# One query-tile loop of sparse attention: GpSimd takes weight scaling from ScalarE, short units share a PSUM bank, scores run on half rows

## The chip, the core and the metric

The kernel runs on one core of a Trainium2 chip. The metric is the device time of one execution in microseconds (us). Five engines work side by side and meet at semaphores: TensorE (PE in the profile, its weight loads as PEld), VectorE (DVE), ScalarE (ACT), GpSimd (POOL) and SyncE (SP), which issues most transfers.

## The reference

A two-layer decoder trunk over 256 tokens of width 1024. The first layer is a gated linear recurrence with a dense SwiGLU; the second is sparse attention with three branches (compressed, selected, window) and a top-2-of-8 expert SwiGLU. Here only the attention of the second layer matters:

```python
lc = einsum('bghqd,bgnd->bghqn', qi, k_cmp) + bias      # compressed keys, 15 of them
o_cmp = masked_softmax(lc, ...) @ v_cmp
ls = einsum(qi, ks) + bias                               # selected blocks: with 256 tokens all of them
o_slc = masked_softmax(ls, dist >= 0) @ vs
lw = einsum(qi, kw) + bias_w                             # window of 512: all earlier tokens
o_win = masked_softmax(lw, ...) @ vw
return gq[..., 0:1] * o_cmp + gq[..., 1:2] * o_slc + gq[..., 2:3] * o_win
```

There are 16 heads of 64 channels in 4 groups; the 4 heads of a group share keys and values. The gates `gq` are sigmoids of a projection of the normed input. The result goes through an output projection (called `mixB` in the kernel), is added to the residual, and the expert layer follows.

## The kernel before, in words

Everything but the expert stage is straight code; each engine has its own instruction list, in an order written by hand, and `then_inc`/`wait_ge` on semaphores are the only ties. PSUM has 8 banks; `job_table` gives each product its bank and its turn in it. `free_bank` waits until the previous job of the bank has been emptied, `filled` waits for a job's product, `evacuated` waits until a job's bank was emptied.

The attention is cut into 32 units `units[u] = (tt, h)`, a head h of one tile of 128 queries. `ORDER` takes the second tile first, so units 0 to 15 are long (256 keys) and units 16 to 31 short (128 keys). For each unit both the selected and the window branch are computed. The steps:

- `scores(u)` on TensorE: one product of 128 rows, `QT[:, h//2]` against `KTZ[h % 2]`. A column block of QT holds two heads, 64 rows each; KTZ[0] has the keys in rows 0 to 63 and zeros below, KTZ[1] (in the tile silu_g) the other way round. The product has 512 columns in a long unit and 256 in a short one. The banks of L rotate over three.
- `biased(s)` on VectorE: the add of the bias out of PSUM into `LB` (line 1486), the row maximum (1489), its sign (1490).
- ScalarE: two exponentials with their sums (1144), one for each branch.
- VectorE: the reciprocal times the gate gives `RW` (1557, 1558, `weight_ready`).
- The scaling of the exponentials by RW: branch 0 on ScalarE (1153), branch 1 on GpSimd (809).
- `turned(u)` on TensorE: 4 transposes of 128 columns in a long unit, 2 in a short one (1913), into job ("PT", u), in banks 2 and 3 by turns.
- ScalarE copies that bank to `PTB` (1160).
- `values(u)` on TensorE for two units at once: the compressed part (`VCZ` against `PCT`), then 16 instructions on 64 columns each in a long pair, 8 in a short one, into the bank of OT. The two heads of a pair go to the two halves of the output rows.

TensorE's list takes units in pairs. In the step for an even s: `scores(s)`, `scores(s+1)`; the compressed scores of a tile if its turn has come (`CMP_AT` is 2 for the long tile and 10 for the short one, here at `CMP_AT - 2`); `turned(s-4)`, `turned(s-3)`; `values(s-6)`. ScalarE's list in step s: both exponentials of unit s, the scaling of unit s-1, the copy of unit s-4. VectorE's: `biased(s)`, compressed work where it is due, the weight of unit s-1.

Ahead of the loop TensorE projects keys, values and queries, sums the query squares (`qsum`), makes the hidden layers of the two compressions (`hid` 0 and 1, of 7.2 us each), the scores of units 0 and 1, the gates' projection (32 products into the bank "gate"), and then small products for the compressed keys (`kc`, `kcsum`) and values (`vc`). VectorE turns the gates into sigmoids (1497, 1498), spreads vc into `VCZ` (1502) and kc into `KCZ` (1511). The compressed scores wait for KCZ (`norm_b`, 5).

After the loop ScalarE moves the last bank of OT (`heads_out`, 912), then, when all four are empty, makes `x_hi` in four pieces (956); VectorE makes `x_lo`; TensorE starts `mixB`, whose first sweep waits for x_hi piece by piece.

Of the kernel before, what the change touches and what calls it, by code (L numbers as in the profile page):

```python
# [29 lines left out]
ALU = mybir.AluOpType  # L30
# [116 lines left out]

def job_table():
# [48 lines left out]
    for br in (1, 2):  # L197
        job(("k", br))
        job(("v", br))
        job(("ksum", br))  # L200
    for b in range(4):
        job(("qB", b))
    for b in range(4):
        job(("qsum", b))
    for s in range(2):
        job(("hid", s))
    job(("gate",))
    job(("kc",))
    job(("vc",))
    job(("kcsum",))  # L210
# [3 lines left out]
    for u in range(TT * HB):  # L214
        job(("L", u), (0, 1, 4)[u % 3])
        job(("PT", u), 2 + u % 2)
# [54 lines left out]
def trunk(nc, ins, out):  # L271
# [5 lines left out]
    with ctx:  # L277
# [89 lines left out]
        VCZ = between[0:ROWS_C, 0, 0:HB // 2 * P].rearrange("p (j n) -> p j n", j=HB // 2)  # L367
        gates = area(15244, TT, 3 * HB)
        qsq = silu_g
        KTZ = [KT, silu_g[:, :, :].rearrange("p (b g) t -> p b g t", b=2)]  # L370
# [355 lines left out]
        def _(pool):  # L726
# [70 lines left out]
            pool.wait_ge(norm_b, 4)  # L797
            for br in range(2):
                pool.dma_start(by_parity(KTZ[1], high, br, 0), by_parity(KT, low, br, 0)).then_inc(keys_copied, 16)
                pool.dma_start(by_parity(KTZ[1], high, br, 1), by_parity(KT, high, br, 1)).then_inc(keys_copied, 16)  # L800
            pool.wait_ge(keys_zero, 1)
            pool.memset(KTZ[1][low], 0.0).then_inc(keys_zero, 1)
            pool.wait_ge(keys_copied, 16 * 6)
            pool.memset(KTZ[0][high], 0.0).then_inc(keys_zero, 1)
# [111 lines left out]
        def _(act):  # L916
# [161 lines left out]
            for br in (1, 2):  # L1078
# [16 lines left out]
                act.activation(ksq[br - 1], ksq[br - 1], ACT.Exp, scale=-0.5).then_inc(rs_b, 1)  # L1095
            for b in range(4):
# [10 lines left out]
            for b in range(4):  # L1107
                evacuated(act, ("qsum", b))
                v = qsq[:, 2 * b:2 * b + 2, :]
                act.activation(v, v, ACT.Exp, scale=-0.5).then_inc(rs_b, 1)  # L1110
            act.preload_act_table_set("gelu_apprx_tanh_and_others")
            for s in range(2):
# [9 lines left out]
                if s == 0:  # L1122
                    for b in (1, 2, 3):
                        refill(make_hi, act, ("qB", b))
            act.preload_act_table_set("natural_log_exp_and_others")
            k = filled(act, ("gate",))
            for tt in range(TT):
                last = act.activation(gates[:, tt, :], ps[:, k, 3 * HB * tt:3 * HB * tt + 3 * HB], ACT.Exp, scale=tok_minus[:, tt:tt + 1])
            last.then_inc(bank_free[k], 1)
# [3 lines left out]
            k = filled(act, ("kcsum",))  # L1133
            act.activation(kcsq, ps[:, k, 0:G * NCMP], ACT.Ln, bias=eps[:, :], scale=1.0 / DH).then_inc(bank_free[k], 1)
            evacuated(act, ("kcsum",))
            act.activation(kcsq, kcsq, ACT.Exp, scale=-0.5).then_inc(rs_b, 1)

            for s in range(len(units) + LAG):
                if s < len(units):
                    w = P * (units[s][0] + 1)  # L1140
                    act.wait_ge(row_max, s + 1)
                    for br in range(2):
                        v = LB[:, s % KEPT, br, 0:w]
                        act.activation(v, v, ACT.Exp, bias=RM[:, s, br:br + 1], accum_out=RS[:, s, br:br + 1]).then_inc(exp_done, 1)  # L1144
                if s in CMP_AT:
# [3 lines left out]
                if 1 <= s <= len(units):  # L1149
# [4 lines left out]
                if s >= LAG:  # L1154
                    u = s - LAG
                    n = 2 * (units[u][0] + 1) * P
                    k = filled(act, ("PT", u))
                    if u >= 4:
                        pv_release(act, u - 4)
                    act.activation(PTB[:, u % 4, 0:n], ps[:, k, 0:n], ACT.Copy).then_inc(bank_free[k], 1)  # L1160
                    if u % 8 == 7 and u > 8:
                        heads_out(act, u // 8 - 1)
            heads_out(act, 3)
            for b in range(4):
                for n in range(4):
# [990 lines left out]
```

## Time and profile before

| what | value |
|---|---|
| median of 3 runs | 1557.31 us (1555.98 to 1561.93) |
| the profiled execution's own time | 1557.5 us |
| its span in the trace | 1555.7 us |
| TensorE / VectorE / ScalarE / GpSimd busy | 96% / 77% / 65% / 9% |
| attention loop, first compressed score to last value product | about 475 to 545.5 us of the span |
| expert stage | from about 590 us to the end |

Times in the rows are microseconds from the start of the span. A busy TensorE is not TensorE at its peak, and the ends of matmuls are modelled; the starts of weight loads tell its pace better. In the chain of work, each row is a piece of the path that ended last, and "x20" is how many instructions were merged.

### The profile page before, as it was taken

The numbers are of one execution on the slowest core, as the hardware profiler recorded it, in microseconds if no ns is written. First come the engines' busy times: TensorE is split into PE (matmuls) and PEld (weight loads), VectorE is DVE, ScalarE is ACT, GpSimd is POOL, SyncE is SP. The second block draws the span as 40 slices with busy tenths as digits, with TensorE's granted clock in tenths as the row PEclk, the third lists the DMA queues.
The fourth block names the chain that finished last, engine by engine and source line by source line (L and its number), as shares of the span: only waits on it lengthen the run. The fifth ranks groups of instructions, "written<-read, shape, count | busy, mean of one in ns | idle before, by whom it ended". The sixth has DMA issues, their size and how long they took to land.

```text
span 1555.7 us, 22749 instructions
## 1 busy us (share of the span) xinstructions
PE 1497.7 (96%) x8592; PEld 1302.9 (84%) x8592; DVE 1199.5 (77%) x1039; ACT 1018.5 (65%) x1005; POOL 141.4 (9%) x145
## 2 busy tenths in 40 slices
PE   8998999999998889999999999999999999999995
PEld 7998899998996687888888888888888888888884
DVE  6854455556457747888888888898898988888887
ACT  5743443435545936778777777777777777777775
POOL 0600100000212309100000000000000000001000
PEclk9999999999998989999999999999999999999998
DMA  9760345556986018999999999999999999999993
GB/s 301 230 204 1 111 163 181 193 177 173 199 245 261 1 55 298 414 399 387 389 375 391 381 373 387 380 375 382 383 381 379 385 372 383 388 373 379 410 376 113
DMA packets 176873, 456.92 MB, mean 294 GB/s; under 512 B 11220, under 2 KB 72877, under 8 KB 176819
## 3 DMA queue, kind: packets, MB, share of 16 engines
q1 hardware_dynamic: 171234, 436.29, 75.9%
q0 software_dynamic: 5408, 19.73, 4.9%
q8 instruction: 38, 0.62, 0.2%
q10 hardware_dynamic: 176, 0.14, 0.0%
q14 instruction: 17, 0.13, 0.0%
HBM read 437.52 MB, written 16.78 MB: 292 GB/s over the span
## 4 chain that ended last, share of the span: by engine, by line
PE 91%; ACT 3%; DVE 2%; DMA 2%; issue 1%; POOL 0%; ACTq 0%; POOLq 0%; DVEq 0%
PE ps L1668 88%; PE ps L2064 2%; DMA ring<-in_moe_w_gu 1%; ACT arena L1144 1%; ACT x_hi L937 0%; PE ps L2130 0%; DVE w_lo L558 0%; DVE arena L1489 0%; DVE arena L1486 0%; DMA arena<-item_rows,arena 0%; ACT between L1160 0%; PE ps L1913 0%; DMA arena<-in_norm_mix_g 0%; ACT arena L1153 0%; ACT w_hi L554 0%
## 5 line engine op out<-in xcount | busy, mean ns | idle before, releaser
L558 DVE TENSOR_TENSOR w_lo<-ring,w_hi 128x2048 fp32r<-128x2048 f32 x339 | 774.0, 2291 | 108.2 <-ACT w_hi L554 107.1
L554 ACT ACTIVATE w_hi<-ring 128x2048 fp32r<-128x2048 f32 x339 | 651.0, 1920 | 237.7 <-PE ps L1668 231.1
L1668 PE MATMUL ps<-w_hi,x_hi 128*128 128x512 f32 (+1 forms) x1056 | 336.9, 383 | 2.7 <-DVE x_lo L1567 2.7
L1668 PE MATMUL ps<-w_hi,x_lo 128*128 128x512 f32 (+1 forms) x1056 | 333.6, 380 | 0.0
L1668 PE MATMUL ps<-w_lo,x_hi 128*128 128x512 f32 (+1 forms) x1056 | 284.0, 380 | 0.0
L1668 PEld LDWEIGHTS ps<-w_hi,x_lo 128*128 128x128 f32 x1056 | 198.7, 188 | 37.6
L1668 PEld LDWEIGHTS ps<-w_lo,x_hi 128*128 128x128 f32 x1056 | 198.6, 188 | 37.6
L1668 PEld LDWEIGHTS ps<-w_hi,x_hi 128*128 128x128 f32 x1056 | 196.3, 188 | 39.5 <-issue 4.4
L507 DVE TENSOR_TENSOR w_lo<-ring,w_hi 128x2048 fp32r<-128x2048 f32 x67 | 153.2, 2291 | 82.4 <-ACT w_hi L501 82.3
L501 ACT ACTIVATE w_hi<-ring 128x2048 fp32r<-128x2048 f32 x67 | 127.5, 1910 | 101.0 <-PE ps L1668 97.7
L1668 PE MATMUL ps<-w_hi,hid 128*128 128x512 f32 x768 | 191.6, 391 | 0.4 <-DVE hid L1625 0.4
L1668 PEld LDWEIGHTS ps<-w_hi,hid 128*128 128x128 f32 x768 | 142.9, 188 | 29.8 <-DVE hid L1625 0.8
L1668 PE MATMUL ps<-x_hi,w_hi 128*128 128x256 f32 x800 | 115.0, 296 | 12.2 <-ACT x_hi L937 6.1
L1668 PEld LDWEIGHTS ps<-x_hi,w_hi 128*128 128x128 f32 x800 | 105.4, 200 | 19.4 <-issue 13.5
L1668 PE MATMUL ps<-x_lo,w_hi 128*128 128x256 f32 x800 | 105.7, 286 | 0.0
L1668 PE MATMUL ps<-x_hi,w_lo 128*128 128x256 f32 x800 | 104.2, 283 | 0.0
L1668 PE MATMUL ps<-w_lo,hid 128*128 128x512 f32 x384 | 102.8, 389 | 0.0
L1668 PEld LDWEIGHTS ps<-x_lo,w_hi 128*128 128x128 f32 x800 | 101.5, 195 | 0.0
L1668 PEld LDWEIGHTS ps<-x_hi,w_lo 128*128 128x128 f32 x800 | 99.6, 192 | 0.1
L1668 PEld LDWEIGHTS ps<-w_lo,hid 128*128 128x128 f32 x384 | 72.1, 188 | 15.0
L889 POOL DMA_DIRECT2D item_rows<-arena x8 | 4.4, 550 | 848.7 <-ACT arena L1225 848.7
L1668 PE MATMUL ps<-hid,w_hi 128*128 128x256 f32 x352 | 63.8, 283 | 0.0
(266 smaller groups left out, 1209.2 us busy)
## 6 DMA issues: line engine op xcount, KB each, us to landing
ring<-in_moe_w_gu SPq DMA_DIRECT2D x224, 1024.0 KB, 6.6
ring<-in_moe_w_down SPq DMA_DIRECT2D x112, 1024.0 KB, 6.6
ring<-in_ffn_w_gu SPq DMA_DIRECT2D x22, 1024.0 KB, 5.1
ring<-in_a_w_in SPq DMA_DIRECT2D x16, 1024.0 KB, 11.3
ring<-in_ffn_w_down SPq DMA_DIRECT2D x11, 1024.0 KB, 5.0
ring<-in_w_kv SPq DMA_DIRECT2D x6, 1024.0 KB, 5.3
item_rows<-hT SPq DMA_DIRECT2D x12, 512.0 KB, 11.7
ring<-in_a_w_out SPq DMA_DIRECT2D x4, 1024.0 KB, 5.4
```

The lines of the kernel that those rows point to most:

```text
L501: eng.activation(w_hi[:, m, :], src, ACT.Copy).then_inc(hi_ready[m], 1)
L507: eng.tensor_tensor(w_lo[:, m, :], ring[:, RAW[name][0], :], w_hi[:, m, :].bitcast(F32), ALU.subtract).then_inc(lo_ready[m], 1)
L554: eng.activation(w_hi[:, m % PAIRS, :], ring[:, m % RING, :], ACT.Copy).then_inc(hi_ready[m % PAIRS], 1)
L558: eng.tensor_tensor(w_lo[:, m % PAIRS, :], ring[:, m % RING, :], w_hi[:, m % PAIRS, :].bitcast(F32), ALU.subtract).then_inc(lo_ready[m % P ...
L889: pool.dma_start(item_rows.ap()[bass.ds(i, 1)].rearrange("o p d -> p (o d)"), yt).then_inc(rows_kept, 16)
L1144: act.activation(v, v, ACT.Exp, bias=RM[:, s, br:br + 1], accum_out=RS[:, s, br:br + 1]).then_inc(exp_done, 1)
L1668: return pe.matmul(o, w, x, start=start, stop=stop, **kw)
L2064: last = pe.transpose(ps[:, b, P * c:P * c + P], HM[:, at:at + P], ident)
```

## The change

1. **Scaling.** `both_on_pool(u)` is true for odd long units and for all short ones. There GpSimd scales both branches and ScalarE none. Even long units stay as they are.
2. **Turned weights.** Two short units share one PT bank (`turned_with`), half a bank each, and ScalarE empties it with one copy of 512 columns instead of two of 256. Banks 2 and 3 alternate between pairs.
3. **Scores.** No zero-padded keys any more. `scores(u)` issues two products of 64 rows, one for each head of a pair, on rows 0 to 63 and 64 to 127, after waiting for both L banks. GpSimd's four key copies are issued in `KT` itself right after the keys are scaled; two memsets of 64 x 2048 and the wait for `norm_b` go.
4. **Gates early.** The gate projection moves ahead of the query projection; its exponential and sigmoid follow there. ScalarE's three weight copies for mixB move ahead of the compression's activations.
5. **Order at the loop's start.** The scores of units 0 and 1 come between the two hidden layers. `biased(0..2)` are interleaved with `make_lo`. KCZ is made at VectorE's step 1, VCZ at step 4. ScalarE's part for kcsum comes after the exponentials of unit 0. Compressed scores are issued at `CMP_AT` instead of `CMP_AT - 2`.
6. **End.** x_hi pieces 0 and 1 are made before the last `heads_out`; TensorE no longer waits for all OT banks.

```diff
+def turned_with(u):
+    return u - u % 2 if ORDER[u // HB] == 0 else u
+def both_on_pool(u):
+    return ORDER[u // HB] == 0 or u % 2 == 1
...
-        job(("PT", u), 2 + u % 2)
+        if turned_with(u) == u:
+            job(("PT", u), 2 + (u // 2 if ORDER[u // HB] == 0 else u) % 2)
...
+                pool.dma_start(by_parity(KT, high, br, 0), by_parity(KT, low, br, 0)).then_inc(keys_copied, 16)
             for u, (tt, h) in enumerate(units):
                 pool.wait_ge(weight_ready, u + 1)
-                v = LB[:, u % KEPT, 1, 0:P * (tt + 1)]
-                pool.tensor_scalar(v, v, RW[:, u, 1:2], None, ALU.mult).then_inc(p2_ready, 1)
+                for br in (0, 1) if both_on_pool(u) else (1,):
+                    v = LB[:, u % KEPT, br, 0:P * (tt + 1)]
+                    pool.tensor_scalar(v, v, RW[:, u, br:br + 1], None, ALU.mult).then_inc(p2_ready, 1)
...
-                if 1 <= s <= len(units):
+                if 1 <= s <= len(units) and not both_on_pool(s - 1):
...
+                    elif u % 2 == 1:
+                        k = filled(act, ("PT", u - 1))
                         pv_release(act, u - 4)
+                        act.activation(PTB[:, u % 4 - 1:u % 4 + 1, 0:T], ps[:, k, :].rearrange("p (u n) -> p u n", u=2), ACT.Copy).then_inc(bank_free[k], 1)
...
+            def scores(u):
+                tt, h = units[u]
+                w = P * (tt + 1)
+                pe.wait_ge(norm_b, h // 4 + 1)
+                for n in range(2):
+                    free_bank(pe, ("L", u + n))
+                for n in range(2):
+                    half, b = slice(DH * n, DH * n + DH), J[("L", u + n)][0]
+                    mm(ps[:, b, 0:2 * w].rearrange("p (b t) -> p b t", b=2), QT[half, h // 2, P * tt:P * tt + P],
+                       KT[half, 0:2, h // HP, 0:w], True, True).then_inc(bank_full[b], 1)
...
+                if s == 0:
+                    pe.wait_ge(keys_copied, 16 * 4)
+                    scores(0)
...
-                    if s == CMP_AT[tt] - 2:
+                    if s == CMP_AT[tt]:
```

## Rows read from the trace of the kernel before

**Rows 1.** The page: the chain that ended last, shares of the span by engine.
```profile
PE 91%; ACT 3%; DVE 2%; DMA 2%; issue 1%; POOL 0%; ACTq 0%; POOLq 0%; DVEq 0%
```

**Rows 2.** Busy time by stretch: PE, PEld, DVE, ACT, POOL, then granted clock, DMA, GB/s.
```profile
475.00:483.00 8.00, 7.93 (x23) 5.03 (x24) 4.59 (x14) 2.74 (x10) 0.94 (x1) 0.57 1.03 419
...
488.00:519.00 31.00, 27.54 (x203) 19.03 (x202) 24.17 (x75) 26.01 (x84) 12.63 (x14) 0.98 0.11 45
519.00:546.00 27.00, 22.18 (x183) 16.65 (x181) 17.34 (x72) 23.75 (x95) 9.07 (x15) 1.00 0.00 1
```

**Rows 3.** The chain of work around the loop's start: start, length, what.
```profile
425.89 45.58 PE ps L1668 x358
...
475.07 4.76 PE ps L1668 x18
```

**Rows 4.** Timeline at the head: start, length, engine, line.
```profile
466.17 0.64 ACT L1119 ACTIVATE arena<-ps 128x240 f32<-128x240 f32 x2 [1.48 <-PE ps L1668]
466.82 1.28 ACT L1125 ACT_TABLE_LOAD   x1
467.79 3.54 PEld L1668 LDWEIGHTS ps<-w_gate,hT 128*128 128x128 f32 x31 [0.24 <-issue]
473.05 1.29 DVE L1502 TENSOR_TENSOR between<-ps,const 120x512 f32<-120x512 f32 x2
474.25 0.56 DVE L1511 SCALAR_TENSOR_TENSOR arena<-arena,cols 64x60 f32<-64x60 f32 x2
```

**Rows 5.** The chain of work among the long units.
```profile
488.30 0.61 DVE arena L1486
...
489.86 1.10 ACT arena L1144 x4
490.96 0.40 ACT arena L1153
491.36 0.49 ACT between L1160
...
491.98 0.63 PE ps L1913 x4
492.61 4.86 PE ps L1668 x38
```

**Rows 6.** Timeline of the same stretch.
```profile
490.00 0.69 DVE L1486 TENSOR_TENSOR arena<-ps,arena 128x512 f32<-128x512 f32 x1
492.76 0.85 PEld L1668 LDWEIGHTS ps<-between,arena 128*64 128x64 f32 x16
494.95 0.69 DVE L1486 TENSOR_TENSOR arena<-ps,arena 128x512 f32<-128x512 f32 x1 [1.27 <-PE ps L1668]
```

**Rows 7.** The chain of work among the short units.
```profile
529.28 0.29 ACT arena L1153
529.57 0.28 ACT between L1160
...
529.98 0.41 PE ps L1913 x2
530.39 1.46 PE ps L1668 x12
531.87 0.44 DVE arena L1486
```

**Rows 8.** Timeline, VectorE, the add of unit 23.
```profile
527.22 0.42 DVE L1486 TENSOR_TENSOR arena<-ps,arena 128x256 f32<-128x256 f32 x1
```

**Rows 9.** Groups by line and form, 488 to 545 us: busy, mean ns, idle before.
```profile
L809 POOL TENSOR_SCALAR arena<-arena 128x256 f32<-128x256 f32 x13 | 12.0, 925 | 18.4 <-DVE arena L1558 18.4
L809 POOL TENSOR_SCALAR arena<-arena 128x128 f32<-128x128 f32 x16 | 9.7, 605 | 14.9 <-DVE arena L1558 14.9
```

**Rows 10.** Timeline behind the last value product.
```profile
545.51 0.60 ACT L912 ACTIVATE xn<-ps 128x512 f32<-128x512 f32 x1 [0.92 <-PE ps L1668]
...
547.43 3.25 PEld L1668 LDWEIGHTS ps<-x_hi,w_hi 128*128 128x128 f32 x14 [0.16 <-ACT x_hi L956]
```

More of the change, by code:

```diff
@@ L200, in job_table @@
         job(("ksum", br))
+    job(("gate",), 5)
     for b in range(4):
@@ L1095, in _ @@
                 act.activation(ksq[br - 1], ksq[br - 1], ACT.Exp, scale=-0.5).then_inc(rs_b, 1)
+            k = filled(act, ("gate",))
+            for tt in range(TT):
+                last = act.activation(gates[:, tt, :], ps[:, k, 3 * HB * tt:3 * HB * tt + 3 * HB], ACT.Exp, scale=tok_minus[:, tt:tt + 1])
+            last.then_inc(bank_free[k], 1)
             for b in range(4):
@@ L1546, in _ @@
                     dve.tensor_copy(PCT[:, tt, :, :], ps[0:ROWS_C, k, 0:T].rearrange("p (a t) -> p a t", a=2)).then_inc(bank_free[k], 1)
-                if 0 < s < len(units):
+                if s == 1:
+                    dve.wait_ge(rs_b, 7)
+                    evacuated(dve, ("kc",))
+                    dve.wait_ge(keys_zero, 1)
+                    for par in range(2):
+                        half = slice(DH * par, DH * par + DH)
+                        last = dve.scalar_tensor_tensor(KCZ[half, :, par, :], KCT[half].rearrange("p (g n) -> p g n", g=G), cols[half, ROW_K:ROW_K + 1],
+                                                        kcsq[half].rearrange("p (g n) -> p g n", g=G), ALU.mult, ALU.mult)
+                    last.then_inc(norm_b, 1)
+                if s == 4:
+                    k = filled(dve, ("vc",))
+                    wide = [ROWS_C, HB // 2, DH]
+                    for a in range(2):
+                        last = dve.tensor_tensor(VCZ[:, 4 * a:4 * a + 4, :].rearrange("p j (r d) -> p (j r) d", r=2),
+                                                 ps[0:ROWS_C, k, DH * a:DH * a + DH].unsqueeze(1).to_broadcast(wide),
+                                                 K("own")[0:ROWS_C].unsqueeze(2).to_broadcast(wide), ALU.mult)
+                    last.then_inc(bank_free[k], 1)
+                if 2 < s < len(units):
                     biased(s)
@@ L1558, in _ @@
                     dve.tensor_tensor(RW[:, u, :], RW[:, u, :], gates[:, tt, 3 * h + 1:3 * h + 3], ALU.mult).then_inc(weight_ready, 1)
-            for n in range(4):
-                evacuated(dve, ("OT", n))
+            pv_release(dve, len(units) - 3)
             input_lo(OT)
@@ L1864, in _ @@
                 mm(ps[:, b, :], halves, ksq[br - 1], True, True).then_inc(bank_full[b], 1)
+            pe.wait_ge(gate_folded, 1)
+            b = free_bank(pe, ("gate",))
+            for tt in range(TT):
+                for k in range(KC):
+                    last = mm(ps[:, b, 48 * tt:48 * tt + 48], hT[:, k, P * tt:P * tt + P], w_gate[:, k, :], k == 0, k == KC - 1)
+            last.then_inc(bank_full[b], 1)
             dense("qB")
@@ L1980, in _ @@
                     values(s - LAG - 2)
-            for n in range(4):
-                evacuated(pe, ("OT", n))
             def logits(ks):
```

142 lines of the change are left out of this document (52 added, 90 removed).

## The prediction

> **What bounds the kernel now.** I read the page first, for the chain that ended last. It is TensorE for nine tenths of the span [rows 1]. So only what lengthens or shortens TensorE's chain counts, and the expert stage, from 590 us on, is untouched: whatever the attention gains arrives at the end one for one, because the expert weights' stream is released by the same chain. Then the chain of work in order of time, which says where TensorE is not alone. Up to the loop's start it is one piece of TensorE work, 45.58 us long [rows 3]. At the start and inside the loop it goes through all four engines. Third, the busy time by stretch: between 488 and 546 us no engine is full. TensorE is busy 27.5 of 31 us and 22.2 of 27, VectorE 24.2 and 17.3, and the granted clock is 0.98 and 1.00 [rows 2]. A loop in which nobody is full is bound by a ring of waits, so I looked for the ring.
>
> **The ring of the long units.** It reads off the chain and the timeline. The add of unit 5 starts at 488.3; its exponentials take 489.86 to 490.96, then ScalarE's queue gives the scaling of unit 4 (0.40) and the copy of unit 1 (0.49) [rows 5]. That copy frees the PT bank for `turned(3)`, at 491.98 (0.63), which is followed in TensorE's list by `values(0)` and `scores(8)`, and the add of unit 8 starts at 494.95 [rows 5, 6]. So three units cost 6.7 us; one more unit of VectorE's own pace is 1.7 us (488.3 to 490.0) [rows 5, 6], and the ring returns to the same parity after 8.4 us for four units, 2.1 us each.
>
> **The ring of the short units** is the same. The add of unit 23 is at 527.22 [rows 8]; the scaling (0.29) and copy (0.28) end at 529.85, `turned` is at 529.98 (0.41), values and scores take 1.46, and the add of unit 26 starts at 531.87 [rows 7]: 4.65 us for three units. VectorE's pace for a short unit I estimate, from the add's 0.44 against 0.69 and the long 1.7 [rows 6, 7], as 1.3.
>
> **The change, part by part.**
>
> *Scaling moved to GpSimd.* ScalarE loses 8 scalings of 0.40 and 16 of 0.29 [rows 5, 7], 7.8 us of work. In a long ring the scaling on the path is that of an even unit (unit 4 above, and it repeats with step 2), and even units keep it on ScalarE. So of the long 3.2 us nothing comes off the path; they were cover only. In the short ring the 0.29 does come off. What is late next is GpSimd: an odd long unit takes 2 x 0.93 = 1.85 us, a short one 2 x 0.605 = 1.21 [rows 9]. The long unit's `turned` then waits for: add of unit 2 places on, + 1.8 for its pace and the weight, + 1.85 + 0.1. Followed by turned, values and scores (3.0, from 491.98 to 494.95 [rows 5, 6]) that is 6.75 us for four units against the ring's 8.4: hidden. In the short ring: 1.3 + 1.21 + 0.1 + 1.9 (529.98 to 531.87 [rows 7]) = 4.5 against about 5.5: hidden too. GpSimd would set the pace only if a scaling took over (8.4 - 6.75)/2 = 0.8 us more than now. Two scalings in a row have no row; I take twice one, with bounds of the same and 1.5 times.
>
> *Shared PT bank.* In short units `turned` of a pair no longer waits for the copy three steps ahead, but `values`, behind it in the same list, still does. So the wait moves over one step: `turned` (0.41) leaves the path, and a copy of 512 columns (0.49 against 0.28 [rows 5, 7]) enters it. With the scaling: 0.29 + 0.41 - 0.2 = 0.5 us for each turn of four units. Sixteen short units are four turns: -2.0 us if all of it counts, 0 if VectorE or GpSimd takes over at once. VectorE is close behind, so I take -1.6.
>
> *Split scores.* Two products of 64 rows replace two of 128. There is no such product in the trace. The nearest row is `values`, where 16 loads on alternating column halves start in 0.85 us, 0.053 each [rows 6], while the four full transposes of a unit take 0.63 [rows 5]. Bounds for a long pair: full overlap saves half of it, none saves nothing; I take overlap of neighbours, a quarter, 0.4 us. The ring waits only for the first product of the pair, and that is not shortened at all. The saving lies in TensorE's slack: worth 0 in the rings, some tenths where TensorE alone is the path.
> The Trainium skill, TensorEngine Tiling (Array Packing), Key Properties, says that tiles work independently, and that changing the tiling mode drains the array. By its first half a long pair would save a half, by the second each pair pays one drain more; on the ring both change the sum by less than 0.5 us, and no row here shows a drain of this kind by itself.
>
> *Compressed scores two units later.* Those of the short tile now stand on the path: the 4.86 us piece with 38 instructions is values(0), two score products and 16 compressed ones [rows 5], of which the 16 are some 1.8. Issued at unit 10 instead of 8, they lie beside VectorE's unit 10 (1.7) and stick out by perhaps 0.5 beyond the two scores ahead of them. -1.3 us, bounds 0 and -1.8.
>
> *Loop start.* The gates' 3.5 us of loads [rows 4] move ahead of the queries: TensorE was the path there and is again, so 0. kc would start at 471.3 as before. But hidden layer 1 now ends last, directly before it: its activation (0.64) and a table load (1.28 [rows 4]), which lay under the gates' products, come onto the path of kcsum. Then ScalarE does unit 0's exponentials (1.1 [rows 5]) before kcsum's two operations, and VectorE adds unit 2 (1.7) before KCZ (0.56 [rows 4]). From 471.3: 0.7 + 1.3 + 0.2 for the square, 0.5 for the kcsum product, 1.1 for scores of unit 2, 1.7, 0.6 gives the compressed scores at 477.4, against 475.07 [rows 3]. There they ran at a granted clock of 0.57 [rows 2] and with two score products took 4.76 [rows 3], after some 2 us of waiting; the new order waits as long, so I take the low clock again: 3.4 for 16, end at 480.9, against 479.8. After that VectorE has unit 2 behind it (-1.6), but VCZ (1.29 [rows 4]) before unit 4. Net 1.1 - 1.6 + 1.3 = +0.8. Bounds: -0.7 if the clock stays up there (16 products at full clock save 1.5), +3 if the third weight copy of mixB, now ahead of the activation in ScalarE's list, waits for its transfer. Half of GpSimd's copies and both memsets go; nothing on the path waited for them.
>
> *End.* Behind the last value product come heads_out at 545.51, x_hi and the first sweep's loads until 550.7, 0.23 each [rows 10]. Four of these 16 products and two x_hi pieces no longer follow heads_out: -1.0, bounds 0 and -2.
>
> **The sum.** +0.8 - 1.3 - 1.6 - 1.0 = -3.1 us. Against the profiled execution's own 1557.5 (span 1555.7 and 1.8 around it), which is 0.2 above the median of the runs, that is 1554.4.
>
> **Rivals.**
> *VectorE's floor.* If relief of ScalarE and TensorE dissolves both rings, VectorE runs without gaps. It idles 6.8 + 9.7 us in the two stretches [rows 2], some 5 of it behind its last unit; 11 less, with +0.8 and -1.0 outside, is -11: 1546.3. For it: the wait between engines is a few tenths in each ring. Against it: the long ring keeps all its links. 0.10.
> *The change does nothing measurable in sum*: the start costs more (up to +3) or GpSimd's pairs and the extra drain eat the short ring's 0.5, -1 to +3 us: 1556.5 to 1560.5. For it: nearly every step leaves a new wait behind the old. 0.23.
> *The clock falls inside the loop* (the other side). TensorE does less in the same time, with more gaps. At 475 to 483 us the clock was 0.57 after such a gap [rows 2]. TensorE's part of each turn of four units is 3.0 us long and 1.9 short [rows 5 to 7]; at half clock it doubles: 11 long units and 16 short ones cost 8.2 + 7.6 = 15.8 more, less the 3.1: up to 1570. It decides when a fifth of the loop (3.1/15.8) runs at 1.2 GHz, and is over 0.5% slower from 0.7 of it on. Against it: now the clock holds at 0.98 to 1.00 with visible gaps. 0.07.
> The Trainium skill, TensorE: Matmul & The Clock Gate, HAM oscillation, has the same mechanism, bursts with waits between them that fall back to the low clock each time; the trace agrees for the loop's start only.
>
> **How the numbers follow.** My forecast, -1 to -7.8 us, has 0.60. The measurement tells 0.5%, 7.8 us, from no change. Faster by more: the floor rival and the forecast's edge, 0.12. Slower by more: the clock rival's worst part, 0.04. Within: 0.84. The range takes the forecast, most of the nothing case and the near end of the floor rival: 1548.5 to 1560.
>
> **What would show it.** In the changed profile: the long ring still 2.1 us a unit with ScalarE idle before the exponentials; short adds about 1.4 us apart; the loop's first four units no earlier than before; unit 10 not delayed by compressed scores; the first mixB product starting before x_hi is whole. Score loads of a pair starting a quarter sooner, not half. GpSimd busy 8 x 0.93 + 16 x 0.605 = 17 us more, never what `turned` waits for. I am wrong if `turned` waits for GpSimd, if VectorE shows no gaps, or if the clock reads below 0.9 between 488 and 540.

## The result: 10 us faster, 7.2 us more than forecast

The changed kernel takes 1547.0 us (median of 11 runs, 1546.4 to 1552.3) against 1557.3 (11 runs, 1554.1 to 1561.9). The ratio is 0.9935, 95% interval 0.9926 to 0.9944: faster by 0.65%. The forecast was 1554.4, its range 1548.5 to 1560.0, with 0.12 for faster by over 0.5%. The time lies outside the range. Eight of the eleven runs lie between 1546.4 and 1547.8, the other three 2 to 5 us above.

The profiled execution's span is 1545.4 us, 10.3 less than before. The table follows the same event through both traces. A step's share is the difference between its own lead and the lead of the row above.

| event (start) | before | after | lead | forecast for the step | measured |
|---|---|---|---|---|---|
| add of unit 5 (loop's start is behind) | 488.2 | 484.7 | 3.5 | +0.8 | -3.5 |
| add of unit 12 (compressed scores behind) | 506.8 | 501.5 | 5.3 | -1.3 | -1.8 |
| add of unit 31 (short ring behind) | 539.1 | 531.5 | 7.5 | -1.6 | -2.2 |
| first of the 64 products behind mixB (the end is behind) | 569.0 | 559.5 | 9.5 | -1.0 | -2.0 |
| end of the span | 1555.7 | 1545.4 | 10.3 | 0 | -0.8 |

Counted from the first piece of x_hi for the queries instead of the span's start, unit 5 came 4.1 us nearer (65.7 us before, 61.6 after): this trace of the changed kernel reached that piece 0.6 us later than the one before.

So three fifths of the error, 4.3 of 7.2 us, were made before unit 5. Read the chain of work there first (start, length, what was on the path):

```profile
414.93 53.78 PE ps L1677 x428
...
468.74 0.63 ACT arena L1128 x2
...
469.39 1.28 ACT L1131
...
470.95 1.50 PE ps L1677 x5
...
472.48 0.70 DVE arena L1497
...
474.66 1.98 PE ps L1677 x16
...
476.67 0.56 DVE arena L1516
```

TensorE now runs in one piece from before 414.93 to 468.71. Before, the piece that I had read as the whole head began at 425.89 [rows 3]. This is the chain of the kernel before just ahead of that row:

```profile
422.19 0.47 ACT arena L1086
422.65 3.19 ACT x_hi L937 x8
```

For 4 us the path went through ScalarE, which made x_hi for the query projection. The busy times of 422 to 426 us say what TensorE did meanwhile (PE, PEld, DVE, ACT, POOL, then clock, DMA share, GB/s), first before, then after:

```profile
422.00:426.00 4.00, 2.23 (x9) 1.01 (x8) 2.45 (x7) 4.00 (x11) 0.00 (x0) 1.00 1.04 348
```

```profile
422.00:426.00 4.00, 4.00 (x33) 3.52 (x32) 2.07 (x6) 3.59 (x10) 0.55 (x1) 1.00 1.04 347
```

One quarter of the loads' time was used, and now nearly all of it: the 32 gate products fall exactly into this hole. From the first x_hi piece to the first query sum it was 25.6 us (422.55 to 448.18) and is 26.4 (423.14 to 449.55). The gates cost 0.8 us in their new place; in the old one they took 3.9 (467.36 to 471.25, the next product).

VectorE at the loop's start (timeline: start, length, idle time in brackets):

```profile
461.45 0.69 DVE L1497 TENSOR_TENSOR arena<-ps,arena 128x512 f32<-128x512 f32 x1 [1.18 <-PE ps L1677]
465.17 0.68 DVE L1497 TENSOR_TENSOR arena<-ps,arena 128x512 f32<-128x512 f32 x1
472.48 0.69 DVE L1497 TENSOR_TENSOR arena<-ps,arena 128x512 f32<-128x512 f32 x1 [3.50 <-PE ps L1677]
```

Units 0 and 1 are done under the second hidden layer, and unit 2 before the compressed scores; the add of unit 3 follows at 478.3 (483.0 before). The adds of units 0 to 2 used to start at 467.7, 474.8 and 479.9.

The granted clock around the compressed scores (474.66 to 476.64 in the changed kernel), first in the changed kernel, then in two of the experiments below, act_scales and copy_first, which have the same order up to there:

```profile
474.00:476.00 2.00, 1.34 (x12) 1.34 (x13) 0.91 (x5) 0.97 (x4) 0.90 (x1) 1.00 1.03 420
```

```profile
474.00:476.00 2.00, 0.12 (x1) 0.12 (x1) 1.89 (x6) 0.68 (x4) 0.00 (x0) 0.63 1.04 424
```

```profile
474.00:476.00 2.00, 0.05 (x1) 0.05 (x1) 1.89 (x6) 0.76 (x4) 0.00 (x0) 0.65 1.03 420
```

In the changed kernel the clock fell as well, but behind the 16 products: it is 0.54 from 476 to 482 us. In the other two it had fallen before them, and they took 3.6 us instead of 2.0.

The stretches of [rows 2] after the change:

```profile
475.00:483.00 8.00, 5.38 (x27) 3.76 (x27) 6.02 (x17) 3.49 (x11) 3.69 (x4) 0.59 1.03 421
488.00:519.00 31.00, 26.51 (x248) 19.23 (x250) 25.80 (x85) 25.00 (x82) 19.83 (x25) 1.00 0.11 42
519.00:546.00 27.00, 22.21 (x183) 16.68 (x182) 16.14 (x60) 17.74 (x60) 14.50 (x25) 1.00 0.00 1
```

Still no engine is full between 488 and 519 us. The long ring has the same links as [rows 5], and its units are no nearer (unit 5 to unit 8: 6.7 us before, 6.8 after):

```profile
486.43 1.09 ACT arena L1141 x4
487.52 0.40 ACT arena L1155
487.92 0.49 ACT between L1162
...
488.54 0.63 PE ps L1925 x4
489.17 2.31 PE ps L1677 x22
```

In the short ring the scaling and `turned` of [rows 7] are gone, and the copy is the long one:

```profile
522.31 0.57 ACT arena L1141 x3
522.88 0.49 ACT between L1166
...
523.51 1.30 PE ps L1677 x11
...
524.83 0.43 DVE arena L1497
```

Behind the loop GpSimd has entered the chain, with the four scalings of the last pair:

```profile
533.02 2.35 POOL arena L812 x4
...
535.50 0.42 PE ps L1925 x2
```

mixB's first loads start before x_hi is whole; the timeline shows two of them, and then the run behind the third piece of x_hi, 10 loads of 0.13 us. Before they took 0.23 [rows 10], at a granted clock of 0.52 (547.43 to 550.68):

```profile
537.87 0.30 PEld L1677 LDWEIGHTS ps<-x_hi,w_hi 128*128 128x128 f32 x2 [0.38 <-issue]
...
540.05 1.26 PEld L1677 LDWEIGHTS ps<-x_hi,w_hi 128*128 128x128 f32 x10 [0.22 <-ACT x_hi L959]
```

From the add of the last unit to that run it is 8.5 us, as before (8.4). The end's 2.0 us come out of the run: four products fewer in it, 0.5, and the rest the clock, which is 1.00 here.

### The profile page after: what moved, and what is told of

Its sections match the earlier page's. It is cut to its first block, busy times and chain, and to the rows that moved or that the text cites. A ratio compares the mean times of both kernels' runs of the same rounds, so it can differ in the third digit from the quotient of the medians.

```text
span 1545.4 us, 22764 instructions
## 1 busy us (share of the span) xinstructions
PE 1486.9 (96%) x8592; PEld 1293.8 (84%) x8592; DVE 1200.6 (78%) x1039; ACT 1010.6 (65%) x973; POOL 152.7 (10%) x165
## 4 chain that ended last, share of the span: by engine, by line
PE 93%; DVE 2%; ACT 2%; issue 1%; DMA 1%; POOL 0%; ACTq 0%; POOLq 0%; DVEq 0%
PE ps L1677 91%; PE ps L2076 2%; DVE arena L1500 1%; DVE arena L1497 0%; PE ps L2142 0%; ACT arena L1141 0%; DMA arena<-item_rows,arena 0%; DMA arena<-in_norm_mix_g 0%; ACT x_hi L940 0%; PE ps L1688 0%; PE ps L1925 0%; ACT x_hi L970 0%; DVE arena L1501 0%; ACT between L1162 0%; POOL arena L812 0%
## 5 line engine op out<-in xcount | busy, mean ns | idle before, releaser
L1677 PEld LDWEIGHTS ps<-x_hi,w_hi 128*128 128x128 f32 x800 | 103.7, 197 | 15.7 <-issue 10.3
```

What stands on the lines that cost most here:

```text
L1677: return pe.matmul(o, w, x, start=start, stop=stop, **kw)
```

## The experiments

Two things make single spans poor witnesses here. The first piece of x_hi for the queries starts between 420.0 and 424.6 us from execution to execution, and what lies behind the stretch used here takes 985.0 to 988.9 us. So I compare the part between: from that x_hi piece to the first of the 64 products behind mixB ("the stretch"), 146.4 us before, 136.4 after. The ratios are to the kernel before, each with its 95% interval. The unit steps are starts of VectorE's adds.

| kernel | median (range, runs) | ratio | stretch, us |
|---|---|---|---|
| gates_late | 1549.2 (1547.4-1551.4, 4) | 0.9939 [0.9916, 0.9962] | 139.5 |
| before_gates_early | 1557.1 (1551.2-1559.5, 10) | 0.9990 [0.9975, 1.0005] | 146.6 |
| before_split | 1558.2 (1556.6-1560.4, 12) | 0.9995 [0.9986, 1.0005] | 148.4 |
| before_split_gates | 1556.1 (1550.8-1558.6, 12) | 0.9979 [0.9962, 0.9996] | 142.9 |
| scores_late | 1553.4 (1551.3-1555.8, 11) | 0.9967 [0.9951, 0.9982] | 142.9 |
| scores_full_late | 1555.0 (1550.9-1558.2, 12) | 0.9973 [0.9956, 0.9990] | 147.5 |
| scores_full | 1566.5 (1565.4-1568.2, 4) | 1.0049 [1.0032, 1.0066] | 157.3 |
| act_scales | 1549.6 (1547.4-1552.3, 4) | 0.9938 [0.9921, 0.9955] | 141.1 |
| pt_alone | 1547.9 (1546.9-1552.2, 4) | 0.9938 [0.9918, 0.9958] | 137.2 |
| cmp_early | 1554.8 (1548.4-1558.3, 10) | 0.9972 [0.9956, 0.9988] | 140.6 |
| tail_old | 1549.9 (1549.5-1551.9, 4) | 0.9949 [0.9932, 0.9965] | 139.4 |
| copy_first | 1548.0 (1541.2-1549.1, 4) | 0.9918 [0.9889, 0.9948] | 134.7 |
| best1 | 1544.3 (1540.6-1546.6, 6) | 0.9907 [0.9891, 0.9923] | 132.1 |
| best2 | 1543.0 (1542.1-1547.1, 6) | 0.9910 [0.9894, 0.9925] | 132.6 |

### The gates, taken out of the change and put alone into the kernel before

gates_late is the changed kernel with the gates' products, exponential and sigmoid behind the hidden layers; before_gates_early is the kernel before with them ahead of the queries (and with the banks that the changed kernel gives the small products around them). The diff shows TensorE's part of the first.

```diff
-            pe.wait_ge(gate_folded, 1)
-            b = free_bank(pe, ("gate",))
...
             dense("qB")
...
+            pe.wait_ge(gate_folded, 1)
+            b = free_bank(pe, ("gate",))
...
             evacuated(pe, ("hid", 0))
```

> The changed kernel with the gates' 32 products, their exponential and their sigmoid put back behind the hidden layers. Theory A (the gates' products fill the gap in which TensorE waits for ScalarE's x_hi pieces at 422 to 426 us, and that is where most of the gain at the loop's start is from): TensorE idles there again and the 3.5 us of loads stand behind the hidden layers again, so 3 to 5 us slower than the changed kernel, 1550 to 1552. Theory B (the gain at the loop's start is from the order of the small steps for the compressed keys, and from the unit sums already made): under 1 us slower, below 1548.

> The kernel before with nothing changed but the gates, whose products, exponential and sigmoid go ahead of the query projection. Theory A: 2.5 to 3.5 us faster than before, 1554 to 1555, with no gap in TensorE's work at 422 to 426 us. Theory B: within 1 us of before.

Taken out of the change, the gates cost 2.8 us up to the first small product behind the hidden layers (kc, 48.1 us behind x_hi instead of 45.3), and that is what the hole at x_hi is worth. The whole stretch is 3.2 us longer. The 0.4 between the two is a balance: the way from kc to the compressed scores is 1.1 us shorter (5.1 for 6.2), and these then took 3.5 us instead of 2.0. By the medians it is 2.2 us, less than the 3 to 5 expected, and the interval of the ratio is too wide to tell it from the changed kernel's 0.9935. Put alone into the kernel before, the gates give nothing (+0.2). The timeline of before_gates_early shows the second bound behind the first:

```profile
466.90 1.80 POOL L804 MEMSET arena<- 64x2048 f32 x1 [5.09 <-DMA silu_g<-arena]
...
468.93 0.30 PEld L1668 LDWEIGHTS ps<-arena 128*128 128x128 f32 x2 [1.56 <-issue]
468.96 1.13 PE L1668 MATMUL ps<-arena 128*128 128x512 f32 x2 [1.46 <-POOL arena L804]
```

TensorE is at `scores(0)` before the zero-padded keys are ready: they wait for a key copy, then a memset. In the kernel before the same memset ended at 465.74, 0.2 us ahead of the scores (465.96), and 0.2 us is also what lies between its end and them here (468.70 to 468.93), so there was nothing to spare. Behind this wait TensorE ran at 0.50 from 470 to 473 us, where the kernel before had 1.00, and the way from kc to the compressed scores took 5.1 us instead of 3.8: the 1.1 us left at kc went there. What follows: the gates' gain needs the new keys as well.

### The split scores, alone and with the gates

before_split is the kernel before with the split scores and their keys; before_split_gates has the early gates as well.

```diff
-        KTZ = [KT, silu_g[:, :, :].rearrange("p (b g) t -> p b g t", b=2)]
...
-            pool.wait_ge(norm_b, 4)
-            for br in range(2):
-                pool.dma_start(by_parity(KTZ[1], high, br, 0), by_parity(KT, low, br, 0)).then_inc(keys_copied, 16)
-                pool.dma_start(by_parity(KTZ[1], high, br, 1), by_parity(KT, high, br, 1)).then_inc(keys_copied, 16)
-            pool.wait_ge(keys_zero, 1)
-            pool.memset(KTZ[1][low], 0.0).then_inc(keys_zero, 1)
-            pool.wait_ge(keys_copied, 16 * 6)
-            pool.memset(KTZ[0][high], 0.0).then_inc(keys_zero, 1)
+                pool.dma_start(by_parity(KT, high, br, 0), by_parity(KT, low, br, 0)).then_inc(keys_copied, 16)
...
-                b = free_bank(pe, ("L", u))
-                mm(ps[:, b, 0:2 * w].rearrange("p (b t) -> p b t", b=2), QT[:, h // 2, P * tt:P * tt + P],
-                   KTZ[h % 2][:, 0:2, h // HP, 0:w], True, True).then_inc(bank_full[b], 1)
+                for n in range(2):
+                    free_bank(pe, ("L", u + n))
+                for n in range(2):
+                    half, b = slice(DH * n, DH * n + DH), J[("L", u + n)][0]
+                    mm(ps[:, b, 0:2 * w].rearrange("p (b t) -> p b t", b=2), QT[half, h // 2, P * tt:P * tt + P],
+                       KT[half, 0:2, h // HP, 0:w], True, True).then_inc(bank_full[b], 1)
```

> The kernel before with only the split scores: two products of 64 rows for each pair, four key copies, no padded keys and no memsets; gates and everything else as before. Theory (split scores and early gates pay only together): alone they save the half of a pair where TensorE is alone on the path, at the loop's start and ahead of the short tile's compressed scores, 0.8 us each, and nothing in the rings: 1555 to 1557 against 1557.3. First mixB load 1 to 2 us nearer to the start of x_hi than the 124.4 of before. Rival (each score product saves by itself in the rings too): 16 pairs at 0.8 and 0.1 us, 4 us or more, under 1553.5.

> The kernel before with the split scores and the early gates, nothing else. The gates alone gave 1557.1 (0.999). Theory (the padded keys were the second bound behind the gates): with both, TensorE neither stands at x_hi nor waits for the keys, so the 3.1 us of the gap at x_hi come on top of the split scores: 1552 to 1554, 3 us below the run with split scores alone, and the first mixB load 4 to 5 us nearer to x_hi's start than in the kernel before. Rival (parts are independent, gates are worth nothing at this place): the same time as with split scores alone.

The distance from x_hi to the first small product behind the hidden layers (kc) is the cleanest measure, because no ring lies in it, and low clock only in before_gates_early's last 0.8 us: 48.7 us before, 47.6 with the gates alone, 48.2 with the split alone, 45.3 with both, 45.3 in the changed kernel. Alone they save 1.1 and 0.5, together 3.4: the coupling is shown there. At mixB it is 5.5 us between the stretches of the split alone and of both, more than the 3 expected; the trace of the split alone has more time at the low clock behind unit 5 (below), and what each wait did to that was not separated. By the ratios the gates alone give 1.6 us, the split alone 0.8 and both 3.3. Only the last is clear of the kernel before, and none of it tells a coupling from a sum.

With the split alone the saving did not reach mixB, and the time did not change: the expected 1 to 2 us nearer fell, the rival's 4 us even more. The trace of before_split has a lower clock where the kernel before has 1.00, and the adds from unit 12 to unit 18 take 15.5 us instead of 12.4:

```profile
504.00:512.00 8.00, 7.38 (x56) 5.37 (x56) 5.85 (x19) 5.78 (x18) 2.77 (x3) 0.79 0.01 2
512.00:519.00 7.00, 5.49 (x38) 4.43 (x39) 3.40 (x13) 5.18 (x19) 2.45 (x3) 0.76 0.01 1
```

### The scores of units 0 and 1 between the hidden layers

scores_late is the changed kernel with the edit below in TensorE's list. scores_full has the padded keys and full products of the kernel before (the split of the last diff undone), with `scores(0)` left between the layers; scores_full_late has both edits.

```diff
-                if s == 0:
-                    pe.wait_ge(keys_copied, 16 * 4)
-                    scores(0)
+            pe.wait_ge(keys_copied, 16 * 4)
+            scores(0)
             evacuated(pe, ("hid", 0))
```

> The changed kernel with zero-padded keys and products of 128 rows again (with the copies and memsets that they need). Theory A (the pair's saving lies in TensorE's slack): 0 to 1 us slower, 1547 to 1548. Theory B (the saving of some 0.8 us for each long pair counts): 16 pairs, 4 to 8 us slower.

> The changed kernel with the scores of units 0 and 1 issued behind hidden layer 1 instead of between the two hidden layers; nothing else. Theory (TensorE is the path up to the small compressed products and the early scores only fill it in another order): the loop's start loses only what VectorE did under hidden layer 1, its add and maximum of units 0 and 1, about 3.5 us of work of which 1 to 2 us come on the path of unit 5: 1548 to 1549. Rival (the order at the start hides the low clock and VectorE's queue altogether): 3 us or more, 1550 and above. First small product (kc) 45.3 us behind x_hi's start as in the changed kernel by both.

> The previous kernel with full products of 128 rows against zero-padded keys (their four more copies and two memsets with them). Compared with the previous one it prices the split scores alone. Theory (half rows save a half of each pair, but in the rings only where TensorE is the path; the padded keys hold TensorE 1 to 2 us at the loop's start): 2 to 4 us above the previous kernel, 1550 to 1553. Rival (split scores are worth what the earlier test showed, 19 us, wherever scores(0) stands): 1562 or more.

scores_late costs 6.5 us of the stretch and 6.4 by the medians (5.0 by the ratios); 5.2 of the 6.5 lie before unit 5. My theory gave 1 to 2 and is wrong; its rival (3 and more) is right. VectorE's timeline says why: with the scores late, it does the adds of units 0 to 2 and two w_lo pieces in one row up to 479 us, and the compressed keys (L1546) stand behind them.

```profile
470.00 0.69 DVE L1497 TENSOR_TENSOR arena<-ps,arena 128x512 f32<-128x512 f32 x1 [8.33 <-PE ps L1677]
...
471.52 2.29 DVE L516 TENSOR_TENSOR w_lo<-ring,w_hi 128x2048 fp32r<-128x2048 f32 x1
...
475.24 2.28 DVE L516 TENSOR_TENSOR w_lo<-ring,w_hi 128x2048 fp32r<-128x2048 f32 x1
...
478.99 0.57 DVE L1546 SCALAR_TENSOR_TENSOR arena<-arena,cols 64x60 f32<-64x60 f32 x2
```

VectorE idled 8.33 us before the first of these rows. From kc to the compressed scores it is 9.7 us (469.89 to 479.61) instead of 6.2 (468.49 to 474.66), and then they run at the low clock, 0.50, after TensorE had waited 7 us.

scores_full_late against scores_late prices the half-row products together with their keys, everything else equal: 4.6 us of the stretch, 2.2 of it before unit 5 (all of it before unit 0: the hidden layers' end waits for the padded keys) and 1.7 between units 5 and 31; by the medians 1.6, by the ratios 0.9, with intervals that overlap. So 1 to 5 us, and that the two kernels differ is not shown by their times. Both expectations for scores_full, 0 to 1 and 4 to 8 us, missed by far: it is 19.5 us slower by the medians. But its 20.9 us of the stretch are no price of the products. In its trace TensorE stands 7.4 us between the hidden layers for the padded keys, and the second layer's 63 loads then take 13.6 us, half the pace, where it is 7.2 in the kernel before; the granted clock from 471.3 to 484.9 us is 0.50:

```profile
467.76 2.05 PE L1685 MATMUL ps<-arena 128*128 128x512 f32 x2 [7.43 <-issue]
...
471.31 13.56 PEld L1685 LDWEIGHTS ps<-arena,ring 128*128 128x128 f32 x63 [0.52 <-issue]
```

The early scores pay only because the unpadded keys are ready then: with padded keys the early ones are worse than the late ones (157.3 against 147.5).

### The short ring: scaling and shared bank

act_scales leaves all scaling of branch 0 with ScalarE (first function); pt_alone gives each short unit its own bank and copy again (second).

```diff
 def both_on_pool(u):
-    return ORDER[u // HB] == 0 or u % 2 == 1
+    return False
 def turned_with(u):
-    return u - u % 2 if ORDER[u // HB] == 0 else u
+    return u
```

> The changed kernel with all scalings of branch 0 back on ScalarE, as before the change; the shared bank, the split scores and the orders stay. Theory A (in short units ScalarE's scaling stands in the ring, in long ones it does not): adds of the short units 0.1 to 0.15 us further apart, 1 to 2 us slower in the loop, but the end behind the last unit shorter by about 1 us since GpSimd's four scalings of the last pair no longer stand on the path: 1547 to 1548. Theory B (ScalarE's relief is what brought both rings down): long units slower too, 1550 or more.

> The changed kernel with one PT bank and one copy for each short unit again. Theory A (the shared bank takes the transposes out of the ring): short adds 0.1 us or more further apart, 1.5 to 2.5 us slower, 1548.5 to 1549.5. Theory B (GpSimd's scaling did it, the bank does nothing): within 0.5 us of 1547.0.

Unit 15 to unit 31 takes 26.2 us before, 24.0 after, 24.9 in act_scales and 25.1 in pt_alone. The parts give 0.9 and 1.1 us, 2.0 of the 2.2 measured. The rest of act_scales' 4.8 us lies where its clock is lower: 1.6 before unit 5 (the 16 compressed scores, above), 1.3 between units 5 and 15 (0.79 between 490 and 498 us) and 0.9 behind unit 31 (0.72 between 538 and 544). There its end was expected 1 us shorter; this trace does not show it. The medians of both lie within the changed kernel's noise.

### The compressed scores

```diff
-                    if s == CMP_AT[tt]:
+                    if s == CMP_AT[tt] - (2 if tt == 0 else 0):
```

> The changed kernel with the short tile's compressed scores issued two units earlier again, as before the change. If their move is worth what the adds of units 8 to 12 suggest (1.8 us), this is 1.3 to 1.9 us slower than the changed kernel, about 1548.7, with the add of unit 10 late by that much. Rival: the move only changed which wait is seen, and the time stays within 0.5 us of 1547.0.

Up to unit 5 nothing differs (61.6 us from x_hi in both). Unit 5 to unit 15 takes 25.5 us instead of 22.8, with a clock of 0.79 from 502 to 510 us (1.00 in the kernel before, with the same order), and unit 15 to unit 31 takes 25.6 instead of 24.0, with 0.73 from 516 to 520. So 1.8 us (from the traces of before and after) is the price at full clock; here it is 4.3 of the stretch, 7.8 by the medians and 5.8 by the ratios. Both expectations missed, the 1.3 to 1.9 us as well as the half microsecond. The clock is what the trace shows beside the order; it was not varied by itself.

### The end

```diff
-            for half in range(2):
-                if half:
-                    heads_out(act, 3)
...
+            heads_out(act, 3)
+            for b in range(4):
+                for n in range(4):
+                    evacuated(act, ("OT", n))
...
+            for n in range(4):
+                evacuated(pe, ("OT", n))
```

> The changed kernel with the old end: x_hi only behind the last heads_out and TensorE's wait for all OT banks. Theory A (the early start keeps TensorE's clock up at the first mixB product): 1.5 to 2.5 us slower, with a granted clock under 0.8 in the first 5 us of mixB. Theory B (only the four products and two pieces count): 0.8 to 1.2 us slower and the clock stays at 1.00.

From the add of unit 31 to the end of the stretch it is 31.0 us, 28.0 in the changed kernel, 29.9 before. The clock from 540 to 546 us is 0.72 here and 1.00 in the changed kernel, and from 532 to 538 it is 0.72 as well. So the new order is worth up to 3.0 us, and theory A is nearer than theory B. With GpSimd's scalings ahead of it, the old order is even slower than in the kernel before. How much of it is the clock and how much the order was not separated.

### The long ring, and two faster versions

copy_first puts ScalarE's copy of unit s-4 ahead of the exponentials of unit s, otherwise unchanged (first lines below). best1 is copy_first with ScalarE scaling branch 0 of the last pair again; best2 is copy_first with GpSimd scaling both branches of every unit up to 29.

```diff
             for s in range(len(units) + LAG):
+                if s >= LAG:
+                    u = s - LAG
...
                 if s < len(units):
                     act.wait_ge(row_max, s + 1)
-    return ORDER[u // HB] == 0 or u % 2 == 1
+    return (ORDER[u // HB] == 0 or u % 2 == 1) and u < 30
+    return u < 30
```

> The changed kernel with ScalarE's copy of the turned weights of unit s-4 put ahead of the exponentials of unit s. If the ring of waits through the PT bank still sets the pace of the long units (2.1 us a unit against VectorE's own 1.8), the tie is cut and the long units come at 1.8 to 1.9 us: 2 to 4 us faster than the changed kernel, 1543 to 1545. Rival: VectorE or the key products take over at once, or the copy then waits for its transposes and holds up the exponentials: between 1 us faster and 1 us slower.

> The changed kernel with ScalarE's copy of unit s-4 ahead of the exponentials of unit s, and the last pair's first branch scaled by ScalarE instead of GpSimd. Theory (the long ring is bound by exponentials, then scaling, then copy; GpSimd ends last behind the loop): the copy ahead gave 1.6 us between x_hi and mixB, the last pair 0.5 to 1 more: 1544 to 1546 against 1547.0. Rival (VectorE and GpSimd already set the pace of the second half, and the clock falls at the start when the loop begins faster): 1547 to 1549, no better than the changed kernel.

> As the previous one, but GpSimd scales both branches of every unit below 30, even long ones too. Theory: with the copy ahead ScalarE's even scaling (0.40 us) is the next link of the long ring; GpSimd needs 1.85 us for a long unit and VectorE's pace is 1.7, so the long ring would be set by GpSimd at about 1.9 us a unit: 0 to 2 us worse than the previous kernel, 1545 to 1548. Rival (ScalarE is the link that counts): 16 units come 0.1 to 0.2 us nearer, 1543 to 1545.

In copy_first unit 5 to unit 8 takes 5.4 us instead of 6.8, and the chain among the long units is VectorE's alone. The adds follow each other at 1.79 us:

```profile
489.47 0.70 DVE arena L1497
490.19 0.70 DVE arena L1500
490.92 0.17 DVE arena L1501
...
491.26 0.70 DVE arena L1497
...
493.06 0.70 DVE arena L1497
```

That shows that the ring of exponentials, scaling and copy bound the long units in the changed kernel, and where the floor lies; in the kernel before, which has the same links and the same 6.7 us, the tie was not cut. Unit 5 to unit 31 takes 43.2 us in copy_first and best1 against 46.8 in the changed kernel, 3.6 less; copy_first gives 1.6 of it back at the start, where its clock fell earlier (unit 5 is 63.2 us behind x_hi, 61.6 in best1 and in the changed kernel). So its stretch is 1.7 us shorter, less than the 2 to 4 expected, and by the medians it is not faster at all (1548.0 against 1547.0, four runs). Scaling the last pair on ScalarE saves 0.7 to 0.9 us more: from the add of unit 31 it is 27.3 us to the end of the stretch, against 28.0 in the changed kernel and 28.2 in copy_first, which had some of the low clock there. So best1 beats the changed kernel by 4.3 us of the stretch, 2.7 by the medians, and the intervals of the ratios do not meet. best2 is as fast: unit 5 to unit 15 is 20.9 us in both. VectorE sets both, so where the even units are scaled no longer matters; its expectation and its rival both named the wrong engine. GpSimd is near its own limit then, 27.2 of 31 us (PE, PEld, DVE, ACT, POOL):

```profile
488.00:519.00 31.00, 27.68 (x258) 19.93 (x256) 28.45 (x97) 24.71 (x87) 27.21 (x36) 1.00 0.07 26
```

## Why the prediction was wrong

**Loop start: +0.8 forecast, -3.5 measured; this step failed.** The end of the long tile's compressed scores was forecast at 480.9 and is 476.64. The links from kc on were right: from kc's start to the compressed scores 6.2 us (468.49 to 474.66), where I had added up 6.1. Two other things were wrong.

First, "TensorE was the path there and is again, so 0" for the gates. I read the chain from 425.89 on, took it for the whole head and missed the hole just before it. kc came 2.8 us earlier (468.49 instead of 471.25). Counted from x_hi it is 3.35, of which gates_late gives 2.8 to the gates and before_split 0.55 to the score pair ahead of kc.

Second, "the new order waits as long, so I take the low clock again". TensorE did wait as long, 2.2 us (472.45 to 474.66), and the clock did fall, but only behind the 16 products: they took 1.98 us instead of the 3.4 assumed. That is 1.4 us; the lower bound of -0.7 was there for it. 2.8 + 1.4 is the 4.3 us of this step but for 0.1. The 1.4 is luck of this execution. Eight kernels have the same order up to there (the changed one, act_scales, pt_alone, cmp_early, tail_old, copy_first, best1 and best2), with kc at 45.3 us and 6.2 us from there to the compressed scores in every trace. In six of the traces the 16 products took 2.0 to 2.1 us, and unit 5 is at 61.6 or 61.7; in act_scales and copy_first they took 3.6, as I had forecast, and it is at 63.2. What decides it was not found, and whether the higher three of the changed kernel's runs are such executions is not known.

**"Half of GpSimd's copies and both memsets go; nothing on the path waited for them."** True of the trace, and still a second failure beside the gates': they ended 0.2 us ahead of their user. before_gates_early shows them as the next bound, scores_full as a 7.4 us stop. A cover of 0.2 us had to be priced, since another part of the same change moved the user forward.

**The early scores** of units 0 and 1 had no term of their own in my sum, whose -1.6 is unit 2's; it took for granted that they were done. Within the new order they carry 6.5 us (scores_late). This is no contradiction to the total: without them the new VectorE order is worse than the old one. The parts of this change are not additive, and my sum treated them as such.

**Split scores: 0 forecast, with a quarter of a pair saved in TensorE's slack.** The size was wrong, the place half right: at the loop's start, where TensorE is the path, the pair was worth 0.55 us. The loads of a long pair and the ones behind it, in the changed kernel:

```profile
460.29 0.30 PEld L1677 LDWEIGHTS ps<-arena 64*128 64x128 f32 x4
461.34 1.75 PEld L1677 LDWEIGHTS ps<-arena,ring 128*128 128x128 f32 x15 [0.76 <-issue]
```

From the pair's first load to the start of the product behind it, it is 1.05 us against 1.82 for a pair before (499.56 to 501.38): 42% saved. The Trainium skill, TensorEngine Tiling (Array Packing), Key Properties, says that tiles work independently, and by that half would be saved; the trace is near it. A short pair, measured the same way, saves a third: 0.64 us (524.09 to 524.73) against 0.96 (525.22 to 526.18).

**Compressed scores, -1.3 forecast, -1.8 measured,** and **short ring, -1.6 and -2.2**: right mechanisms, sized too small. The compressed scores' whole 1.8 us leaves the path, not what sticks out; put back into the changed kernel they cost more than that (cmp_early, 4.3). In the short ring I took off 0.4 for VectorE taking over; it came close (adds 1.3 us apart in a pair) but the full 0.5 for each four units counted. The short ring's "about 5.5" for four units does not follow from its own rows, 4.65 and one unit of 1.3 more make 5.95; nothing in the sum hangs on it.

**End: -1.0 forecast, -2.0 measured.** The four products in advance gave 0.5 of it. The clock behind them, 1.00 instead of 0.52, was not in the sum, nor were GpSimd's four scalings, 2.35 us on the path. The time from the last add to the first run of mixB loads did not shrink (8.5 and 8.4 us); best1, with half of those scalings on ScalarE, ends its stretch 0.7 us nearer to that add.

**The last -0.8** lies behind mixB, within the 4 us by which that part varies between executions. It is not explained.

**The rivals.** VectorE's floor was not reached by the change, but the time came out near it by another way, 1547.0 against 1546.3. copy_first reaches the floor, in the long units. The clock inside the loop, 0.07, did not fall in the changed kernel, but it did in the traces of nine variants: all but gates_late, before_gates_early, pt_alone and the two best have stretches of 6 us or more below 0.85 between 490 and 544 us, in tail_old and copy_first only behind the last unit's add. The Trainium skill, TensorE: Matmul & The Clock Gate, HAM oscillation, describes bursts with waits between them that fall back to the low clock; these nine traces agree, inside the loop too, and the others show no fall there. My sentence that the trace agrees for the loop's start only rested on one trace, and even that one has it again behind the loop, 0.52 from 547.43 on. `turned` waited for GpSimd twice, 0.8 us in all, both times behind the last unit's add.

## What to carry to other kernels

When work is moved, follow the chain back past the place it moves to until the first piece that isn't the moved engine's: a hole of 3 us there is the gain. Then ask what becomes due earlier everywhere behind it, and list the producers that are ready ahead of their user by less than the gain (here 0.2 us). Where parts of a change open places for each other, the price of one undone isn't what it gives alone; test pairs, and align traces at an event, not at the span's start.

## What the runs showed of the hardware that was not expected

The granted clock in one and the same stretch differs between kernels that differ little (504 to 512 us: 1.00 before, 0.79 with the split alone). Units 12 to 18 took 3.1 us more there. What sets it off in one trace and not in the other was not found.

One of VectorE's two-column operations was longer where GpSimd did more beside it. From 488 to 519 us GpSimd was busy 12.6 us before, 19.8 after and 27.2 in best2, and the sign of the row maximum took 173, 184 and 211 ns on average. The reciprocal took 158, 158 and 167, and the 512-column add stayed at 690. Nothing else was held equal between these kernels, so the cause is not shown. Groups by form over the whole loop, before and after:

```profile
L1490 DVE TENSOR_SCALAR arena<-arena 128x2 f32<-128x2 f32 x27 | 4.6, 171 | 0.9
```

```profile
L1501 DVE TENSOR_SCALAR arena<-arena 128x2 f32<-128x2 f32 x28 | 5.6, 200 | 1.0
```

GpSimd scalings in a row cost the same as single ones, 923 ns for 256 columns and 602 for 128 (925 and 605 in [rows 9]):

```profile
L812 POOL TENSOR_SCALAR arena<-arena 128x256 f32<-128x256 f32 x22 | 20.1, 923 | 13.8 <-DVE arena L1568 13.8
L812 POOL TENSOR_SCALAR arena<-arena 128x128 f32<-128x128 f32 x32 | 18.9, 602 | 3.2 <-DVE arena L1568 1.8
```
